# Expert rows scaled by their gates on ScalarE, and added to residual rows in DRAM by an accumulating scatter

## The reference, cut to what matters

```python
def _moe(h, router_w, router_b, w1, b1, w2, b2):     # h = RMSNorm(residual)
    logits = h @ router_w + router_b
    top_v, top_e = lax.top_k(logits, 4)
    gates = jax.nn.softmax(top_v, axis=-1)
    ...                                              # rows grouped by expert in blocks of 128
    def expert_block(args):
        xe, e = args
        a = xe @ w1[e] + b1[e]
        ...                                          # clamped SwiGLU
        return act @ w2[e] + b2[e]
    y = jnp.zeros((N + 1, D)).at[row_tok].add(yb * row_gate[:, None])
    return y[:N]
# _layer:  h = x + mix;  h = h + _moe(_rmsnorm(h, norm2_g), ...)
# then:    y = _rmsnorm(h, normf_g)
```

## Time and profile before

| | us |
|---|---|
| median of 3 runs | 1661.49 (1659.58 to 1664.23) |
| the profiled execution, its time | 1662.83 |
| the profiled execution, its span in the trace | 1660.5 |
| PE busy in the span | 1535.7 (92%) |
| DVE busy | 1222.4 |
| ACT busy | 1004.4 |
| POOL busy | 430.9 |

### The profile page before, as it was taken

The page is one execution under the profiler, slowest core; times in us unless marked ns, Lnnn a source line. Parts: engine busy times, 40 slices in busy tenths (PEclk is TensorE's granted clock), DMA queues, the critical chain, the costliest instruction groups (busy, mean ns, idle before and its releaser), DMA issues.

```text
span 1660.5 us, 23481 instructions
## 1 busy us (share of the span) xinstructions
PE 1535.7 (92%) x7948; PEld 1269.6 (76%) x7949; DVE 1222.4 (74%) x1036; ACT 1004.4 (60%) x894; POOL 430.9 (26%) x398
## 2 busy tenths in 40 slices
PE   6998679996799999999999999999999999999970
PEld 6997445886588888888888888888888888888850
DVE  4323941126688888888888888888888888888858
ACT  4333543014467777777677767776777777677732
POOL 1000000001333223322332333234323322332321
PEclk9998689997899999999999999999999999999995
DMA  8333025322789999999999999999999999999936
GB/s 249 110 104 128 1 77 195 127 108 80 290 316 358 342 359 360 362 361 359 353 365 347 359 359 364 364 354 358 352 352 367 357 363 360 361 362 342 353 129 259
DMA packets 93471, 475.97 MB, mean 287 GB/s; under 512 B 14410, under 2 KB 27354, under 8 KB 43665
## 3 DMA queue, kind: packets, MB, share of 16 engines
q1 hardware_dynamic: 81689, 449.85, 72.3%
q0 software_dynamic: 11744, 25.61, 4.1%
HBM read 468.62 MB, written 23.74 MB: 297 GB/s over the span
## 4 chain that ended last, share of the span: by engine, by line
PE 88%; DVE 8%; DMA 2%; ACT 2%; issue 1%; SPq 0%; POOLq 0%; DVEq 0%; ACTq 0%
PE ps L1632 63%; PE ps L1370 10%; PE ps L1611 3%; PE ps L1637 3%; PE ps L1531 2%; DVE arena L1334 2%; PE ps L1507 2%; DVE lo L957 1%; PE ps L1492 1%; PE ps L1605 1%; DVE arena L1056 1%; DVE stats L1060 1%; PE ps L1533 1%; ACT hi L655 1%; DVE arena L1072 0%
## 5 line engine op out<-in xcount | busy, mean ns | idle before, releaser
L957 DVE TENSOR_TENSOR lo<-raw,hi 128x2048 fp32r<-128x2048 f32 x268 | 605.4, 2289 | 135.6 <-ACT hi L655 135.3
L655 ACT ACTIVATE hi<-raw 128x2048 fp32r<-128x2048 f32 x268 | 498.9, 1910 | 68.0 <-PE ps L1632 61.1
L1632 PE MATMUL ps<-hi,t_hi 128*128 128x512 f32 x1536 | 446.5, 399 | 11.5 <-DVE t_lo L1236 5.2
L1632 PE MATMUL ps<-lo,t_hi 128*128 128x512 f32 x1536 | 434.0, 391 | 0.0
L1632 PE MATMUL ps<-hi,t_lo 128*128 128x512 f32 x1536 | 432.9, 390 | 0.0
L1632 PEld LDWEIGHTS ps<-hi,t_hi 128*128 128x128 f32 x1536 | 279.6, 189 | 75.2 <-DVE lo L957 11.4
L1632 PEld LDWEIGHTS ps<-lo,t_hi 128*128 128x128 f32 x1536 | 289.2, 188 | 62.5
L1632 PEld LDWEIGHTS ps<-hi,t_lo 128*128 128x128 f32 x1536 | 289.0, 188 | 61.0
L957 DVE TENSOR_TENSOR lo<-arena,hi 128x2048 fp32r<-128x2048 f32 x128 | 290.2, 2287 | 20.3 <-ACT hi L655 19.3
L655 ACT ACTIVATE hi<-arena 128x2048 fp32r<-128x2048 f32 x128 | 245.5, 1918 | 45.0 <-PE ps L1632 44.1
L592 POOL COPY idx_g<-idx 128x1 uint32 x30 | 68.9, 2298 | 320.6 <-PE ps L1611 320.6
(11 more groups left out here) (225 smaller groups left out, 1370.8 us busy)
## 6 DMA issues: line engine op xcount, KB each, us to landing
raw<-w SPq DMA_DIRECT2D x256, 1024.0 KB, 5.4
arena<-w SPq DMA_DIRECT2D x128, 1024.0 KB, 7.5
raw<-w_in SPq DMA_DIRECT2D x8, 1024.0 KB, 9.1
raw<-cache_k SPq DMA_DIRECT2D x32, 256.0 KB, 3.6
raw<-cache_v SPq DMA_DIRECT2D x32, 256.0 KB, 3.1
raw<-w_out SPq DMA_DIRECT2D x4, 1024.0 KB, 5.0
arena<-expert_rows SPq DMA_DIRECT2D x2, 2048.0 KB, 13.3
hi<-expert_rows SPq DMA_DIRECT2D x2, 2048.0 KB, 22.1
```

What stands on the lines that cost most here:

```text
L655: act_e.activation(hi[:, slot, :], raw_at(slot_raw), ACT.Copy).then_inc(s_hi, 1)
L957: v.tensor_tensor(lo[:, slot, :], raw_at(slot_raw), hi[:, slot, :].bitcast(F32), ALU.subtract).then_inc(s_lo, 1)
L1632: last = pe.matmul(ps[:, base_bank + b, :], lhs[l][:, row, :], r[:, ck.slot(j), at:at + 512], start=first_k and kk == 0 and q == 0, stop=F ...
```

## The change

`y_dram` gets one row for each token (and 128 spare rows, as `h2_dram` does) instead of one for each token and choice. The residual rows are stored there before the experts start. The index product has four columns instead of two: the token's index and its gate, and the part of each that the rounding of the first two left out. `indices` makes one index and one gate for a slot; an unused slot now has a spare row of its own, so every gather and every scatter moves 128 rows. ACT scales an expert's output by the slots' gates as it copies it from PSUM, and the scatter adds it to the rows in DRAM (`compute_op=ALU.add`). The end loads one finished row for a token, and has no sums. The load of the final norm's weights stands ahead of the wait for the last scatter.

```diff
-UNUSED = 65536.0
+NROWS = NTOK + P
...
-    h2_dram = nc.dram_tensor("h2_rows", [NTOK, D], F32).ap()
-    y_dram = nc.dram_tensor("expert_rows", [NTOK * TOPK, D], F32).ap()
+    h2_dram = nc.dram_tensor("h2_rows", [NROWS, D], F32).ap()
+    y_dram = nc.dram_tensor("sum_rows", [NROWS, D], F32).ap()
...  sync
             sp.wait_ge(s_gat, 16 * (NE + 2))
+            sp.dma_start(raw[:, 3, 0:D], a["normf_g"]...).then_inc(s_gf, 16)
             sp.wait_ge(s_sca, 16 * NE)
-            sp.dma_start(raw[:, 3, 0:D], a["normf_g"]...).then_inc(s_gf, 16)
             for t in FINAL:
                 r, n = TILES[t]
-                sp.dma_start(choices[t][0:n, :], y_rows[r:r + n, :]).then_inc(s_fy[t], 16)
+                sp.dma_start(h_res[0:n, SLOT_H[t], :], y_dram[r:r + n, :]).then_inc(s_fy[t], 16)
...  gpsimd
+            zeros = t_hi[:, :, NTOK:640].bitcast(F32)
+            for rows in (h2_dram, y_dram):
+                for at, n in ((0, 96), (8 * 96, 32)):
+                    spare = rows[NTOK:NROWS, at:at + 8 * n].rearrange("p (k n) -> p k n", k=8)
+                    pool.dma_start(spare, zeros[:, :, 0:n]).then_inc(s_spare, 16)
...
                 pool.dma_start(h2_dram[r:r + n, :], h2[0:n, t % 2, :]).then_inc(s_h2d, 16)
+                pool.dma_start(y_dram[r:r + n, :], h_res[0:n, SLOT_H[t], :]).then_inc(s_hd, 16)
...  make_onehot
-                pool.tensor_copy(vals_c, ...).then_inc(s_pool_c, 1)
+                pool.tensor_copy(vals_c[:, :, 0:2], source).then_inc(s_pool_c, 1)
                 pool.wait_ge(s_pool_c, chain + 2)
+                alone()
+                pool.tensor_tensor(vals_c[:, :, 2:4], source, vals_c[:, :, 0:2].bitcast(F32), ALU.subtract)
...  scatter
                 pool.indirect_dma_start(out=y_dram, out_offset=..., in_=y_sb, in_offset=None,
-                                        bounds_check=NTOK * TOPK - 1, oob_is_err=False).then_inc(s_sca, 16)
+                                        bounds_check=NROWS - 1, oob_is_err=True, compute_op=ALU.add).then_inc(s_sca, 16)
...  scalar, y_out
-                act_e.activation(y_sb, ps[:, 4:6, :]..., ACT.Copy).then_inc(s_ye, 1)
+                act_e.wait_ge(s_gs, m + 1)
+                act_e.activation(slot_g[:], slot_gate[:, bass.ds(gate_column, 1)], ACT.Copy).then_inc(s_act_c, 1)
+                act_e.wait_ge(s_act_c, m + 1)
+                act_e.activation(y_sb, ps[:, 4:6, :]..., ACT.Copy, scale=slot_g[:, 0:1]).then_inc(s_ye, 1)
...  vector, indices
-                v.tensor_scalar(unused[:], ps[:, 6, 0:2], 0.0, UNUSED, ALU.is_equal, ALU.mult).then_inc(s_dve, 1)
+                v.tensor_scalar(unused[:], ps[:, 6, 0:1], 0.0, cst[:, C_SPARE:C_SPARE + 1], ALU.is_equal, ALU.mult).then_inc(s_dve, 1)
+                v.tensor_reduce(slot_gate[:, bass.ds(column, 1)], ps[:, 6, 1:4:2], AX, ALU.add).then_inc(s_gs, 1)
...  vector, end
-            gated_sum(0)
+            v.wait_ge(s_gf, 16)
             for p, t in enumerate(FINAL):
...
-                if p + 1 < NT:
-                    gated_sum(p + 1)
                 v.wait_ge(s_fr, 2 * p + 2)
                 v.reciprocal(st[0:n, 50 + t:51 + t], st[0:n, 50 + t:51 + t]).then_inc(s_fc, 1)
-                if p >= 3:
...
+                v.scalar_tensor_tensor(out=y_fin(t)[0:n, :], in0=h_res[0:n, SLOT_H[t], :], scalar=st[0:n, 50 + t:51 + t],
+                                       in1=raw[0:n, 3, 0:D], op0=ALU.mult, op1=ALU.mult).then_inc(s_fd, 1)
```

More of the change, by code:

```diff
@@ L83 @@
 C_EPS = C_EYE + NE
-NCONST = C_EPS + 1
+C_SPARE = C_EPS + 1
+NCONST = C_SPARE + 1
 def constants():
@@ L179, in build @@
         rank_c = sb("rank_c", [P, NT])
-        unused = sb("unused", [P, 2])
-        idx = sb("idx", [P, TABLE, 2], U32)
+        unused = sb("unused", [P, 1])
+        idx = sb("idx", [P, TABLE], U32)
+        slot_gate = sb("slot_gate", [P, TABLE])
         idx_g = sb("idx_g", [P, 1], U32)
         idx_s = sb("idx_s", [P, 1], U32)
+        slot_g = sb("slot_g", [P, 1])
         cnt = sb("cnt", [1, NE + 8], I32)
@@ L588, in gather @@
                 if isinstance(m, int):
-                    rows = idx[:, column, 0:1]
+                    rows = idx[:, column:column + 1]
                 else:
                     alone()
-                    pool.tensor_copy(idx_g[:], idx[:, bass.ds(column, 1), 0]).then_inc(s_pool_c, 1)
+                    pool.tensor_copy(idx_g[:], idx[:, bass.ds(column, 1)]).then_inc(s_pool_c, 1)
                     rows = idx_g[:, 0:1]
@@ L854, in gated, with y_out @@
                 act_e.activation(act[:, cols], src[:, 0, :], ACT.Gelu_apprx_sigmoid).then_inc(s_s, 1)
-            def y_out(m, done, lin_read):
+            def y_out(m, done, lin_read, gate_column):
                 act_e.wait_ge(s_pc, done)
@@ L885, in body @@
                     if j == 2:
-                        y_out(n - 1, ck.number(0) - PRO, n * 2 + 2)
+                        y_out(n - 1, ck.number(0) - PRO, n * 2 + 2, n - 1)
                 rows_hi(n, s_at, s_ah, act_hi)
@@ L902, in _ @@
                 expert_hi(tail, j)
-            y_out(NE - 2, tail.number(0) - PRO, 2 * NE)
+            y_out(NE - 2, tail.number(0) - PRO, 2 * NE, NE - 2)
             rows_hi(NE - 1, s_at, s_ah, act_hi)
@@ L906, in _ @@
             expert_hi(tail, 3)
-            y_out(NE - 1, PER * NE, 2 * NE)
+            y_out(NE - 1, PER * NE, 2 * NE, NE - 1)
             act_e.wait_ge(s_tab, 3)
@@ L921, in further @@
                     expert_hi(ck, j)
-                y_out(i + NE, ck.number(PER) - PRO, i * 2 + (2 * NE + 2))
+                y_out(i + NE, ck.number(PER) - PRO, i * 2 + (2 * NE + 2), SPARE)
                 act_e.wait_ge(s_sca, i * 16 + 16 * (NE + 1))
@@ L1325, in _ @@
             further_blocks(v, further)
[L1327 to L1338, removed]
-            gated_sum(0)
+            v.wait_ge(s_gf, 16)
             for p, t in enumerate(FINAL):
                 n = TILES[t][1]
-                if p + 1 < NT:
-                    gated_sum(p + 1)
                 v.wait_ge(s_fr, 2 * p + 2)
                 v.reciprocal(st[0:n, 50 + t:51 + t], st[0:n, 50 + t:51 + t]).then_inc(s_fc, 1)
-                if p >= 3:
[L1348 to L1351, removed]
+                v.wait_ge(s_fc, p + 1)
+                v.scalar_tensor_tensor(out=y_fin(t)[0:n, :], in0=h_res[0:n, SLOT_H[t], :], scalar=st[0:n, 50 + t:51 + t],
+                                       in1=raw[0:n, 3, 0:D], op0=ALU.mult, op1=ALU.mult).then_inc(s_fd, 1)
         @block.tensor
@@ L1604, in index_product @@
                 for t in range(NT):
-                    last = pe.matmul(ps[:, 6, 0:2], onehot[:, t, :], vals_c[:, t, :], start=t == 0, stop=t == NT - 1)
+                    last = pe.matmul(ps[:, 6, 0:4], onehot[:, t, :], vals_c[:, t, :], start=t == 0, stop=t == NT - 1)
                 last.then_inc(s_ix, 1)
```

62 lines of the change are left out of this document (25 added, 37 removed).

## The result

The changed kernel takes 1635.12 us in the median of four runs (1633.98 to 1638.82); the kernel before took 1661.24 us beside it. The ratio is 0.9845, with a 95% interval of 0.9824 to 0.9866: 26 us (1.6%) faster, where 1638 us was forecast.

The account below looks back on a forecast made before the run. PE was taken to bound the expert loop at 36.7 us an expert, a separate chain the end. Terms -26.9 + 3 + 0.2 = -23.7 gave 1639.1 from 1662.83, or 1638 us as a median; range 1632 to 1672.

Parts of the forecast that it names:

- The end: Stretch after PE's last work: sums go and loads shrink to one row per token; 26.9 us saved, bounds 22 to 29.5.
- the gates' copy: ACT's copy of 128 gates ahead of the last `y_out`; 0.35 us with its wait.
- the first tile: Load of the first 32 finished rows after the last scatter; 3.0 us instead of 6.94, bounds 2.5 and 4.
- ACT's 1.48 us a tile: Square-sum, read-out and root at the end, with ACT as the chain: first tile 2.85 us, then four times 1.48.
- The scatter's term: Last scatter at the end, now 128 rows and adding: lands in 5.3 us, bounds 3.2 and 9.3.
- DVE's step: Added reduction and register operation before the `lo` PE awaits: 0.1 us per expert, +3 us over 30 experts (0 to 9).
- k = 2: In the expert loop, an accumulating scatter's row costs twice a plain 0.17 us row; 2.6 us added per expert, hidden.
- k = 4.3: Row cost factor where accumulating scatters use up the DMA engines' free 5.8 us per expert; filling them: rival, chance 0.12.
- POOL's cover: Margin, 0.8 us, before POOL's fifth one-hot row slips under DVE's next `lo`; rival: PE stands 1.1 us per expert, chance 0.09.
- The wait for the scatter: In the loop, the scatter lands in about 15 us, hidden; it would bite from 24 us on.
- Ahead of the experts: Larger first gather, changes in `choose`, zeroing spare rows and storing the residual; together +0.2 us, within 1 either way.
- the likeliest case: Whole kernel: the case forecast, 1638 us with its own range of 1632 to 1646; chance 0.62.

Follow-up runs that it names:

- e2: The changed kernel with a last and in-loop scatter that overwrites instead of adding; 1635.89 us.
- e8: The changed kernel with unused slots skipped by gather and scatter, as in the kernel before; median 1634.56 us, ratio 0.983 to the kernel before.
- e1: The kernel before with one sum per tile at the end instead of four, loads unchanged; 1651.43 us.
- e7: The changed kernel with three more two-column reductions on DVE between `unused` and `idx`; 1635.09 us.
- e9: The changed kernel with a second accumulating scatter per expert, issued where POOL is idle before its wait for the expert's output; 1633.76 us.
- e10: The changed kernel with two additional accumulating scatters per expert, issued where POOL is idle before its wait for the expert's output; 1683.76 us.
- e5: The changed kernel with three more 128x10 subtractions on POOL behind the new one; 1637.82 us.
- e6: The changed kernel with eight more 128x10 subtractions on POOL behind the new one; 1666.01 us.

## Why the prediction was right, and where it was off

**The end, -26.9 forecast, -27.4 measured.** Step by step: the gates' copy 0.24 us, and 0.35 with the slower `y_out` behind it, as taken; the last scatter landed in 6.16 us for 5.3, inside its bounds; the first tile in 2.1 us for 3.0; ACT's 1.48 us a tile came out as 1.36, and DVE's reciprocal and product, 1.39 us a tile, rather than ACT, is the chain from the first tile on; the stores 3.1 as before. That the total came within 0.5 us is in part luck: the scatter was 0.9 us too cheap and the first load 0.9 us too dear. The scatter's term had a wrong reason too. It counted eight rows on a DMA engine instead of some four and twice the price for each. The kernel before, e2 and e8 show that 128 rows for 54 are worth little there (4.02 us for 3.21 when plain, 6.16 for 5.65 when adding), and that the addition is worth 2.1 to 2.4 us, 0.5 of it in POOL's issue; a row took 0.43 us of its engine there, over 2.5 times the 0.16 of e2's last scatter (16.8% of 16 engines for 7.7 us, 128 rows). e1 adds what the forecast had only by arithmetic: three quarters of the sums alone gave a third. And the forecast did not name the 6 us for which POOL's products had held up DVE's sums; they went with the sums.

**DVE's step, +3 us forecast (0 to 9), 0 measured.** This is the term that was mis-sized. The reduction went into the hole that the text names, and nothing was left over; I had added 0.1 us for the register operation and the pitch without a row for either. e7 shows that even three more fit.

**The DMA engines: k = 2 taken, 1.9 to 2.1 measured** (0.32 us a row by the share of queue 0, 0.17 for a plain one). The Trainium skill ("Collectives: The Full Stack", "The bandwidth ceiling: the fold count and why AG ≠ RS ≠ AR") has a reduction read two sources and run at half a copy's rate; the rate of this scatter in the loop agrees, 0.32 us a row for 0.17 or 0.16, and no run shows what the engines read. The bound was put at k = 4.3; e9, whose two scatters equal one of k near 4, is free, and e10, near 6, costs 49 us where I reckoned 71. The half of the argument that went by 428 GB/s was the right one; at face value, share 0.95, k = 2 would have been over, and it wasn't. The share stood at 1.00 and there was room for another 2.6 us per expert.

**POOL's cover, 0.8 us reckoned.** e5 (+0.6 us) is inside it, e6 (+1.4 to 1.6) outside, at 1.0 us an expert for the 1.1 forecast. The Trainium skill ("SBUF — State Buffer", "Who interferes with whom") has a DVE instruction with two SBUF inputs contend with a GpSimd instruction that reads SBUF. Both runs agree: in e6 the last one-hot row, which meets DVE's `lo`, ends at 1108.66 us, after `lo` at 1108.20.

**The wait for the scatter.** It lands in 11.0 us in the loop, not 15, with 24 allowed.

**Ahead of the experts, +0.2.** Not separable: executions of the same code differ by more.

**The sum.** It was 3 us too high through DVE's term. That is as much as separates 1638 from 1635.12, but executions of one kernel differ by more (1633.98 to 1638.82), so it needn't be the same 3 us. And the upper end of the likeliest case, 1646, doesn't come out of its parts: with 22 us saved at the end and 9 added by DVE the sum is 1648.7.

## What to carry to other kernels

When two stages of an end run side by side, here the sums on DVE and the loads that feed them, price the end with each of them removed: here fewer sums alone left the loads, and what paid was to take both, even if some work per block goes up in a loop that has room for it. How much room the DMA engines had was told by the sum of the packets' shortest times, not by their busy share, which stood at 1.00 with 8% left. And work moved onto a lightly used engine in a fixed order is judged by what stands behind it there: 1.4 us on POOL, 27% busy, undid the whole gain. It goes the other way as well: POOL's three products at the end of the kernel before stood in the way of DVE's chain, by some 6 us.

## What the runs showed that I had not expected

- Four reductions of two columns cost DVE no more than one: 0.07 us apart, in the 0.45 us that pass between `unused` and the `lo` behind `idx` with or without them.
- The issue of an accumulating scatter holds POOL for 1.6 us (1.57 to 1.65), with 128 rows and, in e8, with the unused ones skipped; the plain scatter of 128 rows in e2 holds it for 1.06 us (1.01 to 1.17).
- Taking 74 of 128 rows out of the last accumulating scatter, with nothing beside it, saves 0.5 us of 6.2.
- The same loads took 89.1% of the DMA engines' time beside one accumulating scatter an expert and 83.5% beside two.
